# Expert loop of a hybrid decoder block: transposes moved from TensorE to VectorE, expert weights loaded in permuted rows, pads skipped by gathers and scatters

## The reference: what is computed

```
p   = RMSNorm(x) @ W_in
A   = gated DeltaNet (4 heads x 128);  B = gated causal convolution + LayerNorm + swish
x   = x + concat(A, B) @ W_out
xn  = RMSNorm(x);  top 4 of 32 experts by a softmax router with bias
for every expert e and its tokens:
    hid  = xn @ w_gate_up[e] + b_gate_up[e]            # 1024 -> 2048
    gate = min(hid[:, :1024], 7);  up = clip(hid[:, 1024:], -7, 7)
    y    = ((up + 1) * gate * sigmoid(1.702 * gate)) @ w_down[e] + b_down[e]
x   = x + sum of the four experts' y, each times its gate
out = RMSNorm(x)
```

## Time and profile before

| | |
|---|---|
| median of 3 runs | 1547.18 us (1546.59 to 1549.49) |
| profiled execution | 1547.54 us, of it 1545.4 us span |
| PE busy | 1383.5 us (90%) |
| DVE, ACT, POOL busy | 585.8, 301.4, 364.7 us (38%, 20%, 24%) |
| DMA | 457.74 MB, mean 296 GB/s |
| granted PE clock, mean | 0.956 of full |

### The profile page before, as it was taken

The page is one execution under the profiler, slowest core; times in us unless marked ns, Lnnn a source line. Parts: engine busy times, 40 slices in busy tenths (PEclk is TensorE's granted clock), DMA queues, the critical chain, the costliest instruction groups (busy, mean ns, idle before and its releaser), DMA issues.

```text
span 1545.4 us, 33728 instructions
## 1 busy us (share of the span) xinstructions
PE 1383.5 (90%) x13158; PEld 643.1 (42%) x13159; DVE 585.8 (38%) x1327; ACT 301.4 (20%) x563; POOL 364.7 (24%) x421
## 2 busy tenths in 40 slices
PE   6998889879758999999999999989999988889982
PEld 2444555555323444434444443533334433334441
DVE  2688888653443222322223222223222223222231
ACT  3113233131201112211212111221112121112122
POOL 5001111010021222332232232323223223222232
PEclk9999999979868999999999999999999999999995
DMA  9212000310267999999999999999999999999994
GB/s 306 75 55 68 15 28 1 113 52 18 105 247 265 349 369 385 404 407 396 410 400 408 408 392 407 401 408 409 406 398 404 409 408 397 408 408 405 408 353 144
DMA packets 110260, 457.74 MB, mean 296 GB/s; under 512 B 15140, under 2 KB 36132, under 8 KB 77430
## 3 DMA queue, kind: packets, MB, share of 16 engines
q1 hardware_dynamic: 86566, 427.88, 69.4%
q0 software_dynamic: 20592, 27.68, 7.6%
q10 hardware_dynamic: 3072, 1.76, 0.4%
HBM read 439.05 MB, written 18.22 MB: 296 GB/s over the span
## 4 chain that ended last, share of the span: by engine, by line
PE 64%; DMA 17%; DVE 11%; SPq 3%; ACT 2%; issue 2%; POOL 0%; DVEq 0%; ACTq 0%; POOLq 0%
PE bank L1828 29%; DMA ring<-in_w_gate_up_dram 16%; PE bank L1870 15%; PE bank L1523 5%; PE bank L1690 4%; PE bank L1896 3%; DVE dslots L974 2%; PE bank L1800 2%; SPq L370 2%; DVE qkbuf L998 1%; SPq L375 1%; PE bank L1589 1%; PE bank L1789 1%; PE bank L1518 1%; DMA rows<-in_x_dram 1%
## 5 line engine op out<-in xcount | busy, mean ns | idle before, releaser
L1828 PE MATMUL bank<-ring,wq 128*32 128x512 f32 x5184 | 587.0, 606 | 40.7 <-DMA ring<-in_w_gate_up_dram 38.5
L1828 PEld LDWEIGHTS bank<-ring,wq 128*32 128x32 f32 x5184 | 163.5, 112 | 414.1 <-issue 413.5
L1870 PE MATMUL bank<-dslots,intra 128*32 128x256 f32 x5056 | 301.7, 381 | 4.3 <-issue 2.1
L1870 PEld LDWEIGHTS bank<-dslots,intra 128*32 128x32 f32 x5056 | 168.1, 110 | 118.3 <-issue 30.6
L857 ACT ACTIVATE wq<-bank 128x512 f32<-128x512 f32 x128 | 66.2, 604 | 628.0 <-PE bank L1828 628.0
L541 POOL DMA_INDIRECT acc_rows<-rows,idx_out x83 | 154.1, 1856 | 45.8 <-POOL idx_out L531 25.6
L1406 DVE TENSOR_TENSOR intra<-bank,small 128x256 f32<-128x256 f32 x128 | 45.4, 418 | 293.7 <-PE bank L1896 261.5
L1523 PE MATMUL bank<-hbuf,ring 128*128 128x512 f32 x320 | 147.2, 601 | 0.0
L1331 DVE TENSOR_TENSOR small<-consts,bank 128x4 f32<-128x4 f32 x34 | 5.4, 159 | 326.3 <-PE bank L1789 326.3
L531 POOL COPY idx_in<-idx 128x4 int32 (+1 forms) x34 | 6.3, 186 | 450.2 <-PE bank L1800 387.9
L536 POOL DMA_INDIRECT wq<-xn_rows,idx_in x88 | 88.2, 1002 | 45.5 <-POOL idx_in L531 27.5
(11 more groups left out here) (274 smaller groups left out, 1067.5 us busy)
## 6 DMA issues: line engine op xcount, KB each, us to landing
ring<-in_w_gate_up_dram SPq DMA_DIRECT2D x256, 1024.0 KB
dslots<-in_w_down_dram SPq DMA_DIRECT2D x124, 1024.0 KB
ring<-in_w_in_dram SPq DMA_DIRECT2D x12, 1024.0 KB
ring<-in_w_out_dram SPq DMA_DIRECT2D x4, 1024.0 KB
ring<-in_w_down_dram SPq DMA_DIRECT2D x4, 1024.0 KB
rows<-in_x_dram SPq DMA_DIRECT2D x4, 512.0 KB, 7.5
hbuf<-in_x_dram SPq DMA_DIRECT2D x4, 512.0 KB, 5.0
xn_rows<-convbuf POOLq DMA_DIRECT2D x4, 512.0 KB, 3.9
```

The source lines that it names most:

```text
L1828: ins = M(bank[g][GROUP * j:GROUP * (j + 1), :], xT[:, g, c % 2, (c // 2) * GROUP:(c // 2 + 1) * GROUP], w[:, :, j * QD:(j + 1) * QD], sta ...
L1870: ins = M(b[GROUP * j:GROUP * (j + 1), col:col + QD], actT[:, g, c % 2, (c // 2) * GROUP:(c // 2 + 1) * GROUP], w[:, cc, j * QD:(j + 1) * QD],
```

## The change

It does four things. **Transposes:** PE's `xt_turn` and `hid_turn` and ACT's `xT_copy` and `hid_copy` go; DVE has one instruction that transposes every 32x32 block of `xg` into `xT` (`xt_turn`), and four that transpose the 32x32 blocks of `bank[g]` into `hidT` (`hid_turn`), both ahead of `act_part`. **Order of rows and columns:** since 32x32 blocks are turned in place, chunk b of the contraction now consists of the rows j*256 + b*32 + s (j of 4, s of 32) of w_gate_up, which is what the load of slot b fetches; and quarter j of the output takes, of every 128 columns, the 32 from 32j on, so that the moving operand is 16 runs of 32 columns. After the turn, hidden unit a*128 + p is on partition p, as w_down has it. **Waits:** POOL's next gather waits for `xt_ready` (DVE) instead of `xt_done` (PE); PE's gate_up waits for `xt_ready`; the `half_read` and `ht_done` semaphores go, and `idx_mm` waits for `idx_ready` of the visit before, since only tables use bank 6. **Pads:** gathers and scatters get a bound, so rows with an index over 2047 are left out.

```diff
@@ -367,7 +367,8 @@ 
             def gate_up(i, c):
                 e = i % E
-                sp.dma_start(view(ring, c * SLOT, SLOT), w_gate_up[0, e, c * P:(c + 1) * P, :]).then_inc(
+                rows_c = w_gate_up[0, e].rearrange("(j b s) n -> b j s n", j=4, b=KC)[c]
+                sp.dma_start(view(ring, c * SLOT, SLOT), rows_c).then_inc(
                     slot_in[c], 16)
@@ -535,13 +536,13 @@ 
                                         in_offset=bass.IndirectOffsetOnAxis(ap=idx_in[:, g:g + 1], axis=0),
-                                        bounds_check=None).then_inc(gathered, 16)
+                                        bounds_check=4 * SEQ - 1, oob_is_err=False).then_inc(gathered, 16)
...
-                                        in_=yb[:, g, :], in_offset=None,
-                                        compute_op=ALU.add).then_inc(scattered, 16)
+                                        in_=yb[:, g, :], in_offset=None, bounds_check=4 * SEQ - 1,
+                                        oob_is_err=False, compute_op=ALU.add).then_inc(scattered, 16)
@@ -585,7 +586,7 @@ 
                 pool.wait_ge(idx_ready, i + 3)
-                pool.wait_ge(xt_done, i + 2)
+                pool.wait_ge(xt_ready, i + 2)
@@ -872,15 +861,8 @@ 
-            act.wait_ge(gu_used, KC)
-            hid_copy()
-            xT_copy(2)
             sigmoid_gate(1)
             with act.Fori(1, m + 2) as i:
-                act.wait_ge(gu_used, i * KC + KC)
-                act.wait_ge(ht_done, i * 2)
-                hid_copy()
-                xT_copy(i + 2)
                 sigmoid_gate(i + 1)
@@ -1314,6 +1296,11 @@ 
+            def xt_turn(visit):
+                dve.wait_ge(gathered, visit * (16 * GROUPS))
+                V.transpose(xT.rearrange("p g n -> p (g n)"), xg.rearrange("p g n -> p (g n)")
+                            ).then_inc(xt_ready, 1)
@@ -1388,32 +1376,33 @@ 
+            def hid_turn(visit):
+                dve.wait_ge(gu_used, visit * KC)
+                for g in range(GROUPS):
+                    V.transpose(hidT[:, g, :, :].rearrange("p h n -> p (h n)"), bank[g][:, :]
+                                ).then_inc(hid_ready, 1)
...
-                for g in range(GROUPS):
-                    V.tensor_tensor(four(g2[:, g, :, :]), four(src[g]), bias(0), ALU.add).then_inc(s, 1)
+                dve.wait_ge(hid_ready, visit * GROUPS)
+
+                def biased(out, half):
+                    bias = bgu[:, half * KC:(half + 1) * KC, bass.ds(e, 1)]
+                    bias = bias.rearrange("p b o -> p (b o)").rearrange("p (b o) -> p b o", o=1)
+                    for g in range(GROUPS):
+                        V.tensor_tensor(out[:, g, :].rearrange("p (b s) -> p b s", b=KC),
+                                        hidT[:, g, half, :].rearrange("p (b s) -> p b s", b=KC),
+                                        bias.to_broadcast([P, KC, GROUP]), ALU.add).then_inc(s, 1)
@@ -1439,6 +1430,8 @@ 
                 lower(e3)
+                hid_turn(i + 1)
+                xt_turn(i + 2)
                 act_part(i % E, i + 1, base + STEPS_IDX)
@@ -1823,11 +1805,10 @@ 
             def gu_mm(c, g):
-                w = view(ring, c * SLOT, 2, D)
+                w = view(ring, c * SLOT, 2 * KC, 4, GROUP)
                 for j in range(4):
-                    ins = M(bank[g][GROUP * j:GROUP * (j + 1), :],
-                            xT[:, g, c % 2, (c // 2) * GROUP:(c // 2 + 1) * GROUP],
-                            w[:, :, j * QD:(j + 1) * QD], start=(c == 0), stop=(c == KC - 1))
+                    ins = M(bank[g][GROUP * j:GROUP * (j + 1), :], xT[:, g, c * GROUP:(c + 1) * GROUP],
+                            w[:, :, j, :], start=(c == 0), stop=(c == KC - 1))
                 return ins
@@ -1858,7 +1840,7 @@ 
                     if not first and c0 == 4:
-                        pe.wait_ge(half_read, i * 2)
+                        pe.wait_ge(idx_ready, i + 2)
                         idx_mm((i + 2) % E, (i + 3) * (T + 1) - 1)
@@ -1887,38 +1868,16 @@ 
             with pe.Fori(1, m + 2) as i:
                 pe.wait_ge(hid_ready, i * GROUPS)
+                pe.wait_ge(xt_ready, i + 1)
                 gate_up(i)
-                pe.wait_ge(idx_ready, i + 3)
-                xt_turn(i * (16 * GROUPS) + 32 * GROUPS)
                 pe.wait_ge(act_ready, i)
                 pe.wait_ge(y_ready, i)
                 tokens = tokens_left(pe, i - 1)
-                down(i - 1, tokens, (0, 1))
-                pe.wait_ge(xt_ready, i + 2)
-                hid_turn(i, 0)
-                down(i - 1, tokens, (2, 3))
-                pe.wait_ge(half_read, i * 2 + 1)
-                hid_turn(i, 1)
+                down(i - 1, tokens, range(4))
```

More of the change, by code:

```diff
@@ L206, in block_kernel @@
         xg = view(wq, 0, GROUPS, QD)
[L207 to L212, removed]
+        xT = view(wq, CAP * 8, GROUPS, KC * GROUP)
+        hidT = view(wq, CAP * 16, GROUPS, 2, KC * GROUP)
+        sg = view(zrows, 0, GROUPS, KC * GROUP)
+        u2 = view(zrows, CAP * 8, GROUPS, KC * GROUP)
+        g2 = view(intra, 0, GROUPS, KC * GROUP)
+        actT = view(intra, CAP * 8, GROUPS, KC * GROUP)
         yb = view(rows, 0, GROUPS, QD)
@@ L266, in block_kernel @@
         gt_done, gt_copied, bd_done, acc_ready = (sem(n) for n in ("gt_done", "gt_copied", "bd_done", "acc_ready"))
[L267 to L270, removed]
+        hot_ready, idx_done, idx_ready, gathered, xt_ready = (sem(n) for n in (
+            "hot_ready", "idx_done", "idx_ready", "gathered", "xt_ready"))
+        gu_used, hid_ready, g2_ready, sg_ready, act_ready = (sem(n) for n in (
+            "gu_used", "hid_ready", "g2_ready", "sg_ready", "act_ready"))
         d_used, y_ready, scattered = sem("d_used"), sem("y_ready"), sem("scattered")
@@ L567, in _ @@
             pool.wait_ge(idx_ready, 2)
-            pool.wait_ge(xt_done, 1)
+            pool.wait_ge(xt_ready, 1)
             fetch_rows(idx_in, 1, 2)
@@ L579, in _ @@
             pool.wait_ge(idx_ready, 3)
-            pool.wait_ge(xt_done, 2)
+            pool.wait_ge(xt_ready, 2)
             fetch_rows(idx_in, 2, 3)
@@ L1367, in _ @@
             dve.sem_inc(route_ready, 1)
+            xt_turn(1)
             hot(1)
@@ L1394, in act_part @@
                 c = base
[L1395 to L1405, removed]
-                    V.tensor_tensor(four(g2[:, g, :, :]), four(src[g]), bias(0), ALU.add).then_inc(s, 1)
+                dve.wait_ge(hid_ready, visit * GROUPS)
[6 more added lines that the diff above has]
+                                        bias.to_broadcast([P, KC, GROUP]), ALU.add).then_inc(s, 1)
+                biased(g2, 0)
                 c = c + GROUPS
                 dve.wait_ge(s, c)
-                dve.sem_inc(half_read, 1)
                 V.tensor_scalar(g2, g2, LIMIT, None, ALU.min).then_inc(g2_ready, 1)
-                dve.wait_ge(ht_done, visit * 2)
-                for g in range(GROUPS):
-                    V.tensor_tensor(four(u2[:, g, :, :]), four(src[g]), bias(1), ALU.add).then_inc(s, 1)
+                biased(u2, 1)
                 c = c + GROUPS
                 dve.wait_ge(s, c)
-                dve.sem_inc(half_read, 1)
                 V.tensor_scalar(u2, u2, LIMIT, -LIMIT, ALU.min, ALU.max).then_inc(s, 1)
@@ L1429, in _ @@
             LOOP_OWN = STEPS_IDX + STEPS_ACT
+            hid_turn(1)
+            xt_turn(2)
             act_part(0, 1, own.n)
@@ L1792, in idx_mm @@
                 ins.then_inc(idx_done, 1)
[L1794 to L1801, removed]
             for t in range(T):
@@ L1849, in gate_up @@
                     if first and c0 == 0:
+                        pe.wait_ge(idx_ready, 1)
                         idx_mm(1, 2 * T + 1)
@@ L1888, in down @@
                     down_mm(u, 1, last).then_inc(d_used, 1)
-            def hid_turn(i, half):
-                if half == 0:
-                    pe.wait_ge(hid_ready, (i + 1) * GROUPS)
-                for g in range(GROUPS):
-                    for hh in range(2):
-                        c = (g % 2) * 256 + hh * P
-                        ins = TR(bank[6 + g // 2][:, c:c + P],
-                                 hid[:, g, half * QD + hh * P:half * QD + (hh + 1) * P], ident)
-                ins.then_inc(ht_done, 1)
             pe.wait_ge(xt_ready, 1)
             gate_up(0, first=True)
-            pe.wait_ge(idx_ready, 3)
-            xt_turn(32 * GROUPS)
-            pe.wait_ge(xt_ready, 2)
-            hid_turn(0, 0)
-            pe.wait_ge(half_read, 1)
-            hid_turn(0, 1)
             with pe.Fori(1, m + 2) as i:
                 pe.wait_ge(hid_ready, i * GROUPS)
+                pe.wait_ge(xt_ready, i + 1)
                 gate_up(i)
-                pe.wait_ge(idx_ready, i + 3)
-                xt_turn(i * (16 * GROUPS) + 32 * GROUPS)
                 pe.wait_ge(act_ready, i)
```

16 lines of the change are left out of this document (3 added, 13 removed).

## The result

The changed kernel takes 3614.84 us (median of 4 runs, 3589.69 to 3637.05) against 1547.42 us before: 2.334 times as long (95% interval 2.323 to 2.345). The forecast was 3416 us. The measured time lies above its own range of 3340 to 3560 and inside the stated range of 3330 to 6000. The profiled execution is the longest of the four, 3637.05 us with a span of 3635.3.

What follows compares the result with a forecast made beforehand. DMA engines bound the loop, PE nearly level. With w_gate_up on four engines, 2875 us for weights and 77 for POOL after 408.7 put the last load at 3361; with the tail 3416 us, own range 3340 to 3560, stated 3330 to 6000.

Steps and rivals of the forecast that it cites:

- the step that decides: Permuted w_gate_up load: outer counts 4 and 128, the smaller rules, so it uses 4 of 16 DMA engines.
- The rate of one engine: Rate of one DMA engine, the middle of the loop's two values 25.5 and 26.3: 25.9 GB/s.
- The term of 2551 us: 252 w_gate_up loads on four engines, 66.1 MB for each at 25.9 GB/s: 2551 us.
- POOL's term: Queue of gathers and scatters: 9.2% of the loop, 97 us, less 20 for pads, 77 us; 2.4 a visit.
- w_down's: 128 w_down loads in the loop on all sixteen engines: 8.4 MB for each engine at 25.9 GB/s.
- the tail: End of the kernel: last gate_up slot lands at 3341, then 5 + 58 + 10 us, span 3414 us.
- the likeliest case: w_gate_up loads on four engines, clean: 3416 us, own range 3340 to 3560, chance 0.48.
- rival 2: Four engines hinder each other writing into SBUF: 5967 us in full step (0.20), 3560 to 5500 partly (0.12).
- The signs: In the loop: DMA share 0.25 to 0.35, 135 GB/s, ring wait over 1000 us, PE under 40%, matmuls 605 ns.
- So they stay full: The four engines never run dry: always 12 MB queued less what PE holds, so the sum is of bytes.
- Rival 1: w_gate_up load stays on sixteen engines: 20 us less for pads, 2 for PE, 1525 us (1510 to 1535), chance 0.17.
- Rival 3: Load on sixteen engines, strided gate_up operand slow: PE bound, 9 us a visit less 3.2, up to 1700 us, chance 0.02.

Runs made afterwards that it cites:

- e4: Kernel before, w_gate_up loaded as 16 blocks of 8 rows, 64 rows (512 KB) apart: four runs from 2007.31 to 2196.79 us.
- e5: Kernel before, w_gate_up loaded as 16 blocks of 8 rows, blocks starting 9 rows (72 KB) apart: 2085.41 and 2168.45 us.
- e7: Changed kernel, w_down loads of the loop cut to 256 bytes a partition (first four and last four whole): 3086.75 us.
- e11: Changed kernel, the loop's w_down loads also taken as 4 blocks of 32 rows of 8 KB: 4268.59 us.
- e1: Changed kernel, w_gate_up load put back to 128 adjoining rows, permutation made where DVE writes the normalised rows: 1528.42 us.
- e9: e1 with the bounds of gathers and scatters taken out, so pads are moved again: 1531.43 us.
- e10: Kernel before with only the bounds on gathers and scatters added: 1542.30 us.
- e8: Changed kernel, each permuted w_gate_up load issued as four loads of 32 rows onto 32 partitions each: 2055.09 us.
- e6: Kernel before, w_gate_up loaded as every eighth row (64 KB apart, 128 rows): 1547.65 us.

## Why the prediction was right, and where it was off

- **The bound and the step that decides.** Right: the spread of the one load over engines, found from a load of 31 rows and one of 32, carries everything. That the smaller of two unlike counts rules was an inference then; 25.1% in a stretch of w_gate_up alone, and 12 and 8 completion packets fewer a load with 4 and 8 blocks, show it. A load of 31 rows was not tried again. So the rule of the Trainium skill (DMA: Bandwidth & Descriptors, section on why a DMA increments its semaphore by 16 and not by 1), the largest number up to 16 that divides both outer counts, holds here in all of its cases tried, 4, 8 and 16 against 128. "The smaller count" would give the same in all three, so these runs don't tell the two apart. The same edit also changes an engine's rate, as e4 and e5 show.
- **The rate of one engine.** 25.9 GB/s taken. Measured 26.6 in the stretch of w_gate_up alone, and over whole visits of e7 (83.05 us less 2.9 for POOL, 2.10 MB for each engine) 26.2, as in e11. The term of 2551 us stands, some 28 us too large. POOL's term is too small: its queue takes 3.0% of 1000 to 3000 us in the changed kernel, 3.0 us a visit instead of 2.4, its 1 KB packets 131 ns on average where e1 has 101.
- **The mis-sized term is w_down's.** "The w_down loads keep all sixteen, 128 x 1.049 / 16 = 8.4 MB", at the same 25.9 GB/s, 10.2 us a visit: the bytes are right, the rate is not. It costs 17.6 us, so the term was 7.4 x 30 = 222 us too small. With POOL's queue some 17 more, w_gate_up's rate 28 less and the tail 16 less (below) that makes 195 of the 221 us by which the profiled span passed the sum (199 between the medians). The rest is not accounted for; 17.6 is itself a difference of medians, and the changed kernel's four runs spread over 47 us. The error of reasoning is that I took an engine's rate from a stretch in which all sixteen share one load pattern, and used it for a mixture of two.
- **The range.** The time of the likeliest case missed its own range by 55 us. The stated range held it because it was stretched to 6000 us for rival 2, where packets of w_gate_up hinder each other; what happened is the mixture with w_down, which had no term, no rival and no chance. That 3614.84 lies inside is owed in part to a range wide enough for another mechanism.
- **The signs.** GB/s (130), the wait for the ring (1987 us) and PE's busy share (36% in the loop) came as forecast. The DMA share was 0.42 in the loop, over the 0.25 to 0.35 given, because packets of both loads take longer while w_down's loads run. The gate_up matmuls were to stay at 605 ns and took 828, though the same list has PE's clock down.
- **"So they stay full."** The four did stay full where it was looked at (25.1%, no gap), but not for the reason given. There were never 12 MB queued: SP is held up in issuing, 8.7 us for each w_gate_up load, and a w_down load lands 34 us after its issue. The queue holds about a third of a visit, which is enough.
- **The tail.** The last gate_up matmuls were taken to begin at 3341 and the span to end 73 us later; in the profiled execution PE begins them at 3577.9, and 57.4 us follow. The 10 us for a half clock weren't needed.
- **Rival 1** (faster, 1525 us) did not happen because its condition failed; e1 makes the condition true and gives 1528.42. Its sum was right by luck: it had 20 us from the pads and 2 from PE, and e9 and e10 show 18 from the transposes and at most 7 from the pads. The fault is the sentence that the DMA engines are the bound "that never lets go", with a share of 1.03 in every stretch: at 1.03 they are, but from 480 to 520 us it is 0.77, at 289 GB/s, and from 520 to 600 us 0.99, at 361 GB/s, with PE busy 79.2 of 80 us and the bound, as e9 shows. The earlier trace rows left those stretches out.
- **Rival 2** (four engines in step, 5967 us) was wrong for this kernel: 309 ns a packet in the stretch with w_gate_up alone. Engines do slow each other in e4, e5 and e8, where sixteen go at 16 to 17 GB/s each by the page, and perhaps in the mixture with w_down; that it is by a shared way into SBUF is not shown.
- **Rival 3** fell: 616 ns for a gate_up matmul in e1. Of the other parts, DVE's transpose out of PSUM was 684 ns for 0.75 us, the one within SBUF 1.20 us for 0.9, a third more than taken and 1.7 times the 695 ns of its nearest row. The PE transposes' 53.94 us stand as 54.2 in the earlier trace rows; nothing hangs on it.

## What to carry to other kernels

Before permuting rows in a load, look at the outermost dimension of both its sides: it sets how many DMA engines run. How fast each of them goes changes too: 128 rows of one distance onto 128 partitions was the only form of the w_gate_up load in which sixteen engines kept their rate. Keep that form, and put a permutation where it is cheap, as in e1, into the output pattern of an operation that writes the data anyway. The number of a queue's completion packets and the DMA share of a stretch with one kind of load tell the engine count directly.

## What the hardware did that I had not expected

- Sixteen engines that load blocks of 8 rows move 15.1 GB/s apiece (e4, 1000 to 1400 us), with the form of the kernel before 25.5; the distance of rows in DRAM, 8, 64, 72 or 512 KB, made no difference between the runs that keep the form (before and e6; e4 and e5).
- Loads of 32 partitions run on all sixteen engines and still at 16.9 GB/s apiece by the page (e8).
- Four engines don't hinder each other at 26.6 GB/s, but they lose 7.4 us a visit of some 92 once w_down's loads run on all sixteen; 8 KB packets near those take 401 ns instead of 313.
- A skipped row of a gather or scatter still leaves its packet: POOL's queue has 20592 packets with the bounds and without, 22.08 MB instead of 27.68. POOL's gather instructions take 1230 ns in the changed kernel instead of 1002, its scatters 1611 instead of 1856, but hardly by the skipping: with the bounds alone (e10) it is 1056 and 1832, with the pads moved and the transposes on DVE (e9) 1213 and 1612. Why the second edit changes them is open.
